# Layer norms of the second block: variance as two columns per token, one spread of the inverted deviation, feature sums begun inside the last unit of the projection ahead

## What is computed

```python
def layer_norm(x, g, b):
    xf = x.astype(jnp.float32)
    mu = jnp.mean(xf, axis=-1, keepdims=True)
    var = jnp.mean(jnp.square(xf - mu), axis=-1, keepdims=True)
    y = (xf - mu) * lax.rsqrt(var + LN_EPS) * g.astype(jnp.float32) + b.astype(jnp.float32)
    return y.astype(x.dtype)

def second_block(x, positions, ...):
    h = layer_norm(x, ln_in_g, ln_in_b)
    for l in range(DEPTH_2):                      # DEPTH_2 = 2
        mix = token_mix(h, ...)                   # ends in merged @ w_o
        h = layer_norm(DEEPNORM_ALPHA * h + mix, ln1_g[l], ln1_b[l])
        ffn = conv_ffn(h, w_up[l], ...)           # ends in ... @ w_down
        h = layer_norm(DEEPNORM_ALPHA * h + ffn, ln2_g[l], ln2_b[l])
    return h
```

## Time and profile before

| | us |
|---|---|
| median of three runs | 2457.18 |
| the profiled execution, its own time | 2455.41 |
| span of the profiled execution, first to last instruction | 2453.6 |
| TensorE busy (94% of the span) | 2314.5 |
| VectorE busy (63%) | 1547.2 |
| ScalarE busy (46%) | 1138.0 |

### The profile page before, as it was taken

How to read it: one execution, slowest core, us unless ns; L and a number is a source line. 1 busy time by engine, 2 the same in 40 slices (tenths; PEclk the granted TensorE clock), 3 DMA queues, 4 the chain that set the end, 5 groups by cost and what they waited for, 6 DMA issues and landing times.

```text
span 2453.6 us, 45807 instructions
## 1 busy us (share of the span) xinstructions
PE 2314.5 (94%) x18358; PEld 2222.9 (91%) x18358; DVE 1547.2 (63%) x2028; ACT 1138.0 (46%) x1477; POOL 345.6 (14%) x448
## 2 busy tenths in 40 slices
PE   8899998999999999999989998978999999889998
PEld 8799997699999999999979998977889988868998
DVE  6846547455467776654775554668677557866763
ACT  4643344543345555433564333535355453445552
POOL 0002100012000000220301210660011019100210
PEclk9999998999999999999999999988999999989999
DMA  7327643166544445565533754434346543424651
GB/s 227 122 75 200 188 143 108 45 167 188 187 152 153 142 152 155 160 188 184 179 107 98 194 189 146 130 103 137 103 139 188 189 137 121 161 69 129 189 189 69
DMA packets 431038, 362.12 MB, mean 148 GB/s; under 512 B 20524, under 2 KB 404144, under 8 KB 430904
## 3 DMA queue, kind: packets, MB, share of 16 engines
q1 hardware_dynamic: 429128, 358.79, 48.1%
q0 software_dynamic: 1264, 0.71, 0.1%
q10 hardware_dynamic: 512, 0.72, 0.1%
HBM read 359.12 MB, written 1.05 MB: 147 GB/s over the span
## 4 chain that ended last, share of the span: by engine, by line
PE 80%; DVE 9%; POOL 6%; ACT 3%; issue 1%; DMA 0%; SPq 0%; ACTq 0%; DVEq 0%; POOLq 0%
PE bank L449 70%; POOL hT L1273 4%; DVE weights_lo L1775 3%; POOL Z L1275 2%; PE bank L480 2%; PE bank L552 2%; PE bank L775 1%; PE bank L789 1%; ACT weights_hi L1311 1%; PE bank L687 1%; PE bank L487 1%; PE bank L905 1%; PE bank L937 1%; DVE negmax L1990 1%; PE bank L918 1%
## 5 line engine op out<-in xcount | busy, mean ns | idle before, releaser
L449 PE MATMUL bank<-h_hi,weights_hi 128*128 128x256 f32 (+1 forms) x3856 | 1103.9, 286 | 53.4 <-DVE weights_lo L1775 17.5
L1775 DVE TENSOR_TENSOR weights_lo<-weights,weights_hi 128x2048 fp32r<-128x2048 f32 x343 | 787.9, 2297 | 552.2 <-ACT weights_hi L1311 549.7
L449 PE MATMUL bank<-h_lo,weights_hi 128*128 128x256 f32 (+1 forms) x3856 | 1093.5, 284 | 0.0
L449 PE MATMUL bank<-h_hi,weights_lo 128*128 128x256 f32 (+1 forms) x3856 | 1092.4, 283 | 0.0
L1311 ACT CAST weights_hi<-weights 128x2048 fp32r<-128x2048 f32 x343 | 654.4, 1908 | 560.5 <-PE bank L449 552.2
L449 PEld LDWEIGHTS bank<-h_hi,weights_hi 128*128 128x128 f32 (+1 forms) x3856 | 742.0, 192 | 63.3 <-issue 49.0
L449 PEld LDWEIGHTS bank<-h_lo,weights_hi 128*128 128x128 f32 (+1 forms) x3856 | 742.2, 192 | 1.5 <-issue 1.4
L449 PEld LDWEIGHTS bank<-h_hi,weights_lo 128*128 128x128 f32 (+1 forms) x3856 | 741.3, 192 | 0.0
L449 PE MATMUL bank<-hid_hi,weights_hi 128*128 (+1 forms) x1056 | 296.8, 281 | 0.0
L449 PE MATMUL bank<-hid_hi,weights_lo 128*128 (+1 forms) x1056 | 296.8, 281 | 0.0
L449 PE MATMUL bank<-hid_lo,weights_hi 128*128 (+1 forms) x1056 | 296.8, 281 | 0.0
(11 more groups left out here) (299 smaller groups left out, 2467.7 us busy)
## 6 DMA issues: line engine op xcount, KB each, us to landing
weights<-in_f_w_gu SPq DMA_DIRECT2D x176, 512.0 KB, 5.0
weights<-in_f_w_out SPq DMA_DIRECT2D x88, 512.0 KB, 4.2
weights<-in_w_up SPq DMA_DIRECT2D x88, 512.0 KB, 4.9
weights<-in_w_in SPq DMA_DIRECT2D x82, 512.0 KB, 4.5
weights<-in_c_w_qkv SPq DMA_DIRECT2D x72, 512.0 KB, 4.5
weights<-in_a_w_qkv SPq DMA_DIRECT2D x48, 512.0 KB, 4.6
weights<-in_w_down SPq DMA_DIRECT2D x44, 512.0 KB, 4.2
weights<-in_a_w_o SPq DMA_DIRECT2D x16, 512.0 KB, 4.0
```

The source lines that it names most:

```text
L449: mm = nc.tensor.matmul(out, x, y, start=(first and n == 0), stop=(last and n == 2), skip_group_check=True)
L1775: v_.tensor_tensor(w_lo[slot][:], raw[slot][:], w_hi[slot][:].bitcast(F32), ALU.subtract).then_inc(lo_ready, 1)
```

## The change

Three edits. First, `deep` gets an argument `summed`; with it, in the last unit, TensorE makes the mean's sums over feature tiles 0 and 1 behind m = 4 and those over 2 and 3 behind m = 6 (`sum_pair`), each behind a wait for the add of that bank. The other two pairs stay in `ln`. It is on for the two `w_o_2` and the two `w_down_2`; the norm on input keeps `sums`. Second, the sums of squares are made by 16 matmuls of one column (128 x 2) in place of 8 of 256 columns. Third, the square root and the reciprocal are taken on 128 x 2, TensorE spreads the result over the partitions into a bank of PSUM, and the multiplication by the gain (L2217) reads the bank instead of SBUF.

```diff
+            def sum_pair(source, j):
+
+                at = 0 if source[0].bank else 4
+                if j == 0:
+                    mean[0] = open_item(at)
+                pe.wait_ge(bank_free[source[j].bank], source[j].free)
+                for k in (2 * j, 2 * j + 1):
+                    mm = nc.tensor.matmul(banks[at][:, 0:T], ones[:], xT[:, k, :], start=(k == 0), stop=(k == KT - 1))
+                if j == 3:
+                    close(mm, mean[0])
...
                         if between and m == 3:
                             between(n, 0)
+                        if summed and last and m in (4, 6):
+                            sum_pair(out, m // 2 - 2)
                     close(mm, u, *([out[3]] if last else []))
...
                 at = 0 if source and source[0].bank else 4
                 if source:
-                    m = sums(at, xT, lambda j: pe.wait_ge(bank_free[source[j].bank], source[j].free))
+                    for j in (2, 3):
+                        sum_pair(source, j)
+                    m = mean[0]
                 else:
                     m = sums(at, xT, lambda j: pe.wait_ge(y_ready, 2 * j + 2))
-                v = sums(at + 1, sq, lambda j: pe.wait_ge(squares_ready, count(squares_ready)))
+                v = open_item(at + 1)
+                for k in range(KT):
+                    if k % 2 == 0:
+                        pe.wait_ge(squares_ready, count(squares_ready))
+                    for tt in range(NT):
+                        mm = nc.tensor.matmul(banks[v.bank][:, tt:tt + 1], sq[:, k, tt * P:(tt + 1) * P], ones[:, 0:1],
+                                              start=(k == 0 and tt == 0), stop=(k == KT - 1), skip_group_check=True)
+                close(mm, v)
+                pe.wait_ge(rs_ready, count(rs_ready))
+                r = open_item(at + 2, released=False)
+                close(spread(at + 2, 0, 0), r)
...
-                whole_deviation(v, D, 1, sq[:, 0, :])
+                deviation(v, ((0, 2, D),), 1)
...
-                link(v_.reciprocal(sq[:, 1, :], sq[:, 0, :]))
+                v_.reciprocal(rs[:, 0:2], std[:, 0:2]).then_inc(rs_ready, 1)
+                done(r)
...
-                        v_.scalar_tensor_tensor(hT[:, k, :], xT[:, k, :], pcol[:, at + k:at + k + 1], sq[:, 1, :],
-                                                ALU.mult, ALU.mult).then_inc(ln_ready, 1)
+                        v_.scalar_tensor_tensor(hT[:, k, :], xT[:, k, :], pcol[:, at + k:at + k + 1],
+                                                banks[r.bank][:, 0:T], ALU.mult, ALU.mult).then_inc(ln_ready, 1)
```

More of the change, by code:

```diff
@@ L564, in rotation, with deep @@
                                        pre[x.pre][lo:hi, 0:n], start=True, stop=True), r)
-            def deep(name, l, n_units, src, tag, bank0, ready, looped=False, between=None):
+            mean = [None]
+            def sum_pair(source, j):
[7 more added lines that the diff above has]
+                    close(mm, mean[0])
+            def deep(name, l, n_units, src, tag, bank0, ready, looped=False, between=None, summed=False):
                 head, loop, tail = [], [], []
@@ L627, in deep, with wo @@
                 items[tag, "units"] = head, loop, tail
-            def wo(name, l, tag, bank0, src_items=None, src=h, between=None):
+            def wo(name, l, tag, bank0, src_items=None, src=h, between=None, summed=False):
                 base = None if src_items else count(h_ready, 4) - 4
@@ L639, in wo @@
                 flat = [x[:].rearrange("p m n -> p (m n)") for x in src]
-                deep(name, l, 4, flat, tag, bank0, ready, between=between)
+                deep(name, l, 4, flat, tag, bank0, ready, between=between, summed=summed)
             def ffn(name_up, name_down, l, tag):
@@ L677, in ready @@
                     pe.wait_ge(hidden_ready, hid0 + 2 * n + 2 if i is None else i * 6 + (hid0 + 2 * n + 2))
-                deep(name_down, l, 11, (hid_hi, hid_lo), (tag, "down"), 0, ready, looped=True)
+                deep(name_down, l, 11, (hid_hi, hid_lo), (tag, "down"), 0, ready, looped=True, summed=tag[0] == "ffn2")
             def transposes(hd, plan, expos):
@@ L982, in ln @@
                 if source:
-                    m = sums(at, xT, lambda j: pe.wait_ge(bank_free[source[j].bank], source[j].free))
+                    for j in (2, 3):
+                        sum_pair(source, j)
+                    m = mean[0]
                 else:
                     m = sums(at, xT, lambda j: pe.wait_ge(y_ready, 2 * j + 2))
-                v = sums(at + 1, sq, lambda j: pe.wait_ge(squares_ready, count(squares_ready)))
+                v = open_item(at + 1)
[9 more added lines that the diff above has]
+                close(spread(at + 2, 0, 0), r)
                 count(ln_ready, KT)
-                items[tag] = m, v
+                items[tag] = m, v, r
             def mix(l):
@@ L1113, in mix @@
                      lambda n, i: pe.wait_ge(bank_free[O[n].bank], O[n].free))
-                wo("w_o_2", l, (tag, "wo"), 4)
+                wo("w_o_2", l, (tag, "wo"), 4, summed=True)
                 items["m", l] = it
@@ L1599, in ln @@
             def ln(tag, last):
-                m, v = items[tag]
+                m, v, r = items[tag]
                 fn(tiny[:], eps[:, 0:1], ACT.Sqrt)
```

## The result

The changed kernel takes 2468.1 us in the median of 20 runs, the kernel before, run beside it, 2457.3 in 20: +10.8 us, a ratio of 1.0045 with a 95% interval of 1.003 to 1.006. Single runs of either spread over some 17 to 22 us. Of the later comparisons, one execution of the kernel before at 4377 us and one of a filled kernel at 5284 us are left out. The profiled execution of the changed kernel took 2467.35 us with a span of 2465.4, 11.8 above the span of before.

The account below looks back on a forecast made before the run. TensorE, busy 94% of the span, was taken as the bound, with a serial chain of waits through each norm. Terms +4.7 - 2.5 - 0.3 + 7.0 = +8.9 us gave 2465 us, range 2456 to 2474.

Parts of the forecast that it names:

- Edit one: At four projections, mean's sums moved into the last unit: gain 0, since TensorE sets the end; cost +4.7 us.
- The stall: Ahead of the first pair of moved sums, TensorE waits for VectorE's first add: 1.55 to 1.59 us at three projections.
- The last add: Bank 7's add at the projection's end runs beside the third pair of sums: hidden, or 0.1 us over.
- From the root on: Root to first multiplication in five norms: 2.29 us becomes 1.78, -2.5 us; with a full-clock spread 1.27, bound -5.1.
- The columns: Sums of squares in five norms: -0.3 us at full clock, +7.0 (0 to 14) for clock falls; blocks 3.6 to 6.4.
- The first products: Behind four norms, already at half clock, costing 6.0 us in all; change put at 0, with 2 us either way.
- fell early: Rival: the clock falls early in all five column blocks, +16.2 us, 2472.5 us; chance 0.12.
- the fourth: Rival: at the projections the adds come early enough, so moved sums cost 0; +4.2 us, 2460.5 us; chance 0.10.
- The faster rival: The spread's matmuls break the idle stretch, so the clock never falls in blocks or products: -6.7, 2449.6 us; chance 0.08.
- The reading by busy time: In the column blocks, columns count like wide matmuls for the clock gate and lose nothing; given rival 3's chance.
- rival 3: The faster rival: clock never falls in the column blocks or first products, -6.7, 2449.6 us; chance 0.08.
- rival 1: The clock holds through the column blocks: -0.7 us, 2455.6 us, no change; chance 0.20.

Follow-up runs that it names:

- filled kernel: Any kernel given extra wide matmuls, into a bank nobody reads, in TensorE's idle time within the norms; series ratios from 0.9958 to 1.0002.
- both fills: Kernel before with 3 wide matmuls ahead of the sums of squares and 8 behind them, in five norms; 0.9962, then 0.9967.
- the one behind alone: Kernel before with only the 8 wide matmuls behind the sums of squares, none ahead; 0.9978, then 0.9965 to 0.9991 aside, 0.9958 in the second series.
- columns filled: Changed kernel with the mean's sums unmoved, plus wide matmuls: 3 ahead of the column block, 1 behind it, 3 behind the spread; 0.9977 of before.

## Why the prediction was right

The forecast was +8.9 us and 2465, the change of the medians +10.8 us, and 2468.1 lies in the range. By its own steps:

- **Edit one gains nothing.** Shown from both sides: alone it costs 7.8 us, and without its stall the stretch to the centring is still 0.1 to 0.2 us longer than before at each of the four.
- **The stall.** 1.55 to 1.59 us forecast at three projections and none at the fourth; the trace has idle time of 1.50 to 1.52 at the three and none at the fourth. That is from the modelled end of a product; by starts, which the forecast used, it is 1.67 at the first `w_o_2`. From VectorE's end (1774.91 + 0.69) to TensorE's start 0.14 us pass, where 0.05 was taken. Moving the weight unit away took the stall away.
- **The last add.** Called hidden, or 0.1 us over. From the first sum at 1775.74 to the centring at 1781.76 the changed kernel takes 6.02 us; the 18 products (2.10 us) and the eight sums with the start of the centring (1779.26 to 1782.91 before, 3.65) need 5.75. So it was 0.27 here and 0.2 at the last projection, some 1.0 us in all. Edit one cost 6.0 us in the trace where 4.7 were forecast: its two terms were mis-sized.
- **From the root on.** 1.78 us forecast, 1.78 measured (1787.02 to 1788.80), with the spread of 1.22 us at half clock in all five norms. The full-clock chain did not occur.
- **The columns.** The forecast was +6.7 us for all five, the middle between never and early, with -0.3 in it for full clock. The trace has 26.6 against 18.5, +8.2. The blocks of 6.55 and 6.33 us lie round the upper bound of 6.4 (the fall came 0.5 and 0.7 us in, not 0.8), that of 3.73 at the lower one; the filled kernels show that the 1.5 us of idle time ahead does bring the fall forward, as the argument had it. How far is not forecast by anything in it: the same blocks gave +8.2, +9.2 and +5.3 in three traces, so the middle was a fair mean, and that one trace lies near it is in part luck. One reading was wrong: the trace of before has ten such blocks, seven of 3.6 to 4.0 us, and not in all of them did TensorE come straight from wide matmuls. Ahead of two of 3.73 us it stood idle for 0.69, and there is this one:

```profile
704.93 4.82 PE L480 MATMUL bank<-ones,sq 128*128 128x1 f32 x32 [1.99 <-ACT sq L1359]
```

With 2.0 us of idle time ahead it is the row nearest to a layer norm. Its 4.82 us against the 3.69 of the wide sums, five times, would have made +5.6 for the columns.

- **The first products.** Put at 0 with 2 us either way. The changed kernel's trace has +0.7 behind the multiplication. In the kernel before the low clock is worth 4.3 us at the four projections and 0.8 at the output's transposes, where the prediction's rows gave 6.0 for the four.
- **The rivals.** The clock did not hold through the blocks (only one of five) and it fell early in two of five, not in all. The adds did not come early, as the fourth needed. The faster rival needed the spread's two matmuls to keep the clock; they ran at half clock in all five norms. That the first products can keep the clock is right, but what kept it was 3.6 us of wide matmuls in an idle stretch of 4.1; less was not tried on the kernel before. The reading by busy time, under which the blocks lose nothing, was given rival 3's chance; it is as much the condition of rival 1, and fell with both.

Summed with the measured sizes: 6.0 for edit one, 8.2 for the columns, -2.6 for the chain, 0.7 for the products and 0.6 for the clock at the norm on input make +12.9 in the five norms; the rest of the kernel, whose code is unchanged, took 1.0 less: 11.8 in the spans. No term was saved by an error of another; all but the chain came out somewhat larger than forecast.

## A version that beats both

The kernel before with TensorE's idle time in the norms filled. Its four series, two with both fills and two with the one behind alone, give 0.9962, 0.9967, 0.9978 and 0.9958 of before; all four intervals lie under 1. Whether columns and fills together are better still is open: in the traces the columns filled gain 7.3 us in the norms against 5.0 to 5.9 of these four, since the shorter chain (-2.8) outweighs the blocks (+0.9), but its one series, 0.9977, lies at the upper end of theirs.

## What to carry to other kernels

Work that is moved into another engine's stream takes its wait along: before moving it, compare when the stream gets there with when the producer ends, and ask whether a wait bounded the old place at all. Fewer columns were not less time here, where each matmul loads its own 128 columns of weights (3.73 us against 3.69), and the clock fell in and behind them. Where a serial stretch on other engines leaves TensorE idle, spare wide matmuls in it can be worth more than shortening the stretch: 5.1 us in the norms against 2.6.

## What was not expected of the hardware

One-column matmuls that kept TensorE busy all the time did not keep its clock: behind 1.5 us of idle time it fell to 0.50 early enough to lengthen four of five blocks of the changed kernel; with 0.24 us ahead and three wide matmuls among the columns it fell in four of five too. The Trainium skill, TensorE: Matmul & The Clock Gate, section What's actually happening, lets the gate go by how busy the engine was; read as busy time the traces disagree, with 5.9 us of nearly full busy time at clock 0.50. What the gate counts was not settled. And identical code ahead of the second block took from 6.0 us less to 5.3 us more than in the trace of before; its cause was not looked for.
